# Diffusion step in fp32 on one core: the first layer's latent projection in two halves of the features, woven into the loading of the modulation blocks, and three unread products in place of nine

## The reference

```python
mod_s = jnp.split(modulation(c, w_mod[layer], b_mod[layer]), MOD_CHUNKS, -1)    # silu(c) @ w_mod + b_mod
hs = modulate(rms_norm(xs, g_norm1[layer]), mod_s[0], mod_s[1])                 # h * (1 + scale) + shift
proj = h @ w_in                                  # layer 0: 256 + 128 + 32 latent columns, then 2 x 512 of the conv branch
cq, ckv, k_rope, glu = proj[..., :256], proj[..., 256:384], proj[..., 384:416], proj[..., 416:]
```

## Time and profile before

| what | us |
|---|---|
| median of 3 runs | 1579.98 |
| lowest and highest run | 1578.2, 1583.39 |
| the profiled execution, its own time | 1586.21 |
| its span (the first to the last instruction) | 1584.0 |
| TensorE busy | 1442.6 (91%) |
| VectorE, ScalarE, GpSimd busy | 807.4, 474.6, 201.6 |
| mean granted clock of TensorE | 0.973 of full speed |
| DMA | 268.68 MB, mean 170 GB/s |

### The profile page before, as it was taken

How to read it: one execution, slowest core, us unless ns; L and a number is a source line. 1 busy time by engine, 2 the same in 40 slices (tenths; PEclk the granted TensorE clock), 3 DMA queues, 4 the chain that set the end, 5 groups by cost and what they waited for, 6 DMA issues and landing times.

```text
span 1584.0 us, 34040 instructions
## 1 busy us (share of the span) xinstructions
PE 1442.6 (91%) x14714; PEld 1016.4 (64%) x14714; DVE 807.4 (51%) x1586; ACT 474.6 (30%) x1066; POOL 201.6 (13%) x201
## 2 busy tenths in 40 slices
PE   3999989999999998778898999988989999999994
PEld 2555567745588886556676776766755444788883
DVE  1278678734443433535566665665644525343432
ACT  2201655512100000544554544554531202000000
POOL 2200020100312121131011010110100002112111
PEclk9999999999999999889998998999999999999998
DMA  9764573232899999522101201111012433999994
GB/s 344 263 224 134 171 244 123 79 120 102 294 344 345 338 342 352 160 72 56 45 22 46 64 22 46 45 42 59 6 57 74 156 106 142 318 341 344 338 291 112
DMA packets 165158, 268.68 MB, mean 170 GB/s; under 512 B 7697, under 2 KB 107289, under 8 KB 164337
## 3 DMA queue, kind: packets, MB, share of 16 engines
q1 hardware_dynamic: 149008, 206.29, 38.5%
q0 software_dynamic: 16000, 60.23, 13.0%
HBM read 237.45 MB, written 36.36 MB: 173 GB/s over the span
## 4 chain that ended last, share of the span: by engine, by line
PE 75%; DVE 9%; issue 5%; DMA 4%; ACT 3%; DVEq 1%; SPq 1%; POOL 0%; ACTq 0%; POOLq 0%
PE psum L1679 14%; PE psum L928 9%; PE psum L2125 8%; PE psum L1690 7%; PE psum L580 5%; PE psum L2187 4%; PE psum L2137 2%; PE psum L334 2%; PE psum L2684 2%; PE psum L1392 2%; PE psum L489 2%; PE psum L1671 2%; PE psum L944 2%; DMA arena<-in_w_mod 1%; PE psum L955 1%
## 5 line engine op out<-in xcount | busy, mean ns | idle before, releaser
L2125 PE MATMUL psum<-hT,ring 128*128 128x384 f32 (+1 forms) x736 | 241.9, 453 | 1.0 <-ACTq L213 0.7
L2125 PEld LDWEIGHTS psum<-hT,ring 128*128 128x128 f32 x736 | 128.3, 194 | 34.5 <-issue 2.1
L1679 PEld LDWEIGHTS psum<-arena,ring 128*128 128x128 f32 x1152 | 131.1, 192 | 12.4 <-issue 10.4
L1679 PE MATMUL psum<-arena,ring 128*128 128x128 f32 x1152 | 131.9, 275 | 4.8 <-DVE arena L1720 4.8
L1758 DVE TENSOR_TENSOR arena<-arena,psum 128x256 f32<-128x256 f32 x34 | 14.3, 421 | 211.7 <-PE psum L1679 211.7
L737 DVE SCALAR_TENSOR_TENSOR arena<-arena,params_sb 128x655 f32<-128x655 f32 x120 | 106.1, 906 | 5.6
L2187 PEld LDWEIGHTS psum<-arena 32*32 32x32 f32 x5120 | 55.7, 111 | 65.3 <-issue 37.6
L2187 PE MATMUL psum<-arena 32*32 32x32 f32 x5120 | 64.9, 200 | 29.6 <-issue 18.5
L1620 POOL DMA_INDIRECT ysum<-arena,small x34 | 53.9, 1587 | 285.5 <-DVE arena L1728 284.9
L1741 ACT ACTIVATE arena<-psum 128x256 f32<-128x256 f32 x34 | 13.1, 384 | 222.6 <-PE psum L1679 222.6
L928 PE MATMUL psum<-ring,arena 128*128 128x512 f32 x160 | 72.6, 608 | 1.0 <-ACTq L213 1.0
(11 more groups left out here) (476 smaller groups left out, 2626.8 us busy)
## 6 DMA issues: line engine op xcount, KB each, us to landing
arena<-in_w_mod SPq DMA_DIRECT2D x18, 1024.0 KB, 5.2
ring<-in_m_w_gate SPq DMA_DIRECT2D x18, 1024.0 KB, 11.2
ring<-in_m_w_up SPq DMA_DIRECT2D x18, 1024.0 KB, 16.8
ring<-in_m_w_down SPq DMA_DIRECT2D x18, 1024.0 KB, 15.1
ring<-in_w_mod SPq DMA_DIRECT2D x17, 1024.0 KB, 5.5
modN<-in_m_w_down SPq DMA_DIRECT2D x16, 1024.0 KB, 15.9
ring<-in_c_w_in SPq DMA_DIRECT2D x24, 512.0 KB, 6.7
arena<-in_m_w_gate SPq DMA_DIRECT2D x8, 1024.0 KB, 13.6
```

Source lines behind the costliest of these rows:

```text
L1679: m = pe.matmul(bank((2, 4)[half] + (1, 3)[half] * q, P, f * P), gu_slot[s][:, c0:c0 + P], xgT[:, q, k, :], start=(k == 0), stop=(k == KC ...
L2125: m = pe.matmul(bank(un % 2, w), ring[:, s, c0k:c0k + P], hT[:, k, o:o + w], start=(k == 0), stop=(k == KC - 1))
```

## The change

1. The order of the loads: blocks 0 and 2 of the modulation weights (shift and scale of the features 0 to 511), then the latent weights of those features (0.85 MB), then blocks 1 and 3, then the other half of the latent weights. The latent weights have a slot of their own, so they no longer wait for a product.
2. TensorE multiplies blocks 0 and 2 and turns them into columns, then transposes tiles and multiplies the first four feature chunks of each tile (`latent_half(pe, t, 0)`). The products of blocks 1 and 3 and the columns from them are put in between. The other four chunks follow for all five tiles at the end. Each tile accumulates in a bank of its own, 0 to 4.
3. The first half of a tile is modulated out of PSUM by ScalarE (even tiles) or VectorE (odd tiles); the other engine copies the second half into `hT` as it is. When the second half of `mcol` is there, VectorE modulates it in place, chunk by chunk over all 640 rows: 8 instructions, with one count of `mod_k` for each chunk.
4. All five `latent_copy` stand behind the barrier `norm0a`, which TensorE now reports to in the midst of its products.
5. `unread_products` in the combination: 3 in place of 9.

Semaphore totals and reused semaphores are adapted. Nothing else of the 1584 us is touched.

```diff
@@ mod_sp
-            for b in range(NCB):
-                sp.dma_start(first_slot[b].rearrange("p (k n) -> p k n", k=KC), w[:, :, b * 512:(b + 1) * 512]).then_inc(S(f"mod_w{b}"), 16)
+            for half, sem in enumerate(("in0_w_lat", "in0_w_u")):
+                for b in (half, 2 + half):
+                    sp.dma_start(first_slot[b].rearrange("p (k n) -> p k n", k=KC), w[:, :, b * 512:(b + 1) * 512]).then_inc(S(f"mod_w{b}"), 16)
+                sp.dma_start(ring[:, 0, 4 * half * LAT:4 * (half + 1) * LAT].rearrange("p (k n) -> p k n", k=4),
+                             w_in[:, 4 * half:4 * half + 4, 0:LAT]).then_inc(S(sem), 16)
@@ mod_pe
-            for b in range(NCB):
-                if b == NCB - 2:
-                    norm_tile_pe(pe, 0, 0)
-                    norm_tile_pe(pe, 0, 1)
-                pe.wait_ge(S(f"mod_w{b}"), 16)
-                block_rows(pe, first_slot[b], bank(6, P, b * P), 0, KC).then_inc(S("mod_col_mm"), 1)
-            rows_to_columns(pe, 0)
-            arrive(pe, "pe")
+            first_rows(pe, 0)
+            first_rows(pe, 2)
+            rows_to_columns(pe, 0, (0, 2), 2)
@@ norm0_act
-            act.wait_ge(S("mod_col_mm"), NCB)
-            act.copy(col_rows[0], bank(6)).then_inc(S("mod_vec_ev"), 1)
+            act.wait_ge(S("mod_col_mm"), 2)
+            act.copy(halves(col_rows[0])[:, :, 0, :], halves(bank(6))[:, :, 0, :]).then_inc(S("mod_vec_ev"), 1)
...
+            for t in range(NT):
+                act.wait_ge(S("norm_tr"), 2 * t + 1 + t % 2)
+                if t % 2:
+                    m = act.copy(hT_half(t, 1), bank(late_bank(t)).rearrange("p (a b) -> p a b", a=4))
+                else:
...
+            act.wait_ge(S("mod_col_mm"), 4)
+            act.copy(halves(col_rows[0])[:, :, 1, :], halves(bank(6))[:, :, 1, :]).then_inc(S("mod_vec_ev"), 1)
@@ norm0_dve
+            mod_columns(dve, 0, (1,), 3)
+            dve.wait_ge(S("in_hT_act"), NT)
+            dve.drain()
+            for k in range(4, KC):
+                for c, part in ((0, slice(0, P)), (1, slice(P, T))):
+                    m = dve.tensor_scalar(hT[:, k, part], hT[:, k, part], mcol[:, 0, 1, k, c:c + 1], mcol[:, 0, 0, k, c:c + 1], ALU.mult, ALU.add)
+                m.then_inc(S("mod_k"), 1)
@@ norm_pe
+            first_tile_pe(pe, 0)
+            first_tile_pe(pe, 1)
             pe.wait_ge(S("in0_w_lat"), 16)
-            for t in range(NT):
-                latent_product(pe, t)
-                if t + 2 < NT:
-                    norm_tile_pe(pe, 0, t + 2)
+            latent_half(pe, 0, 0)
+            first_tile_pe(pe, 2)
+            latent_half(pe, 1, 0)
+            first_tile_pe(pe, 3)
+            first_rows(pe, 1)
+            latent_half(pe, 2, 0)
+            first_tile_pe(pe, 4)
+            first_rows(pe, 3)
+            latent_half(pe, 3, 0)
+            rows_to_columns(pe, 0, (1, 3), 3)
+            arrive(pe, "pe")
+            latent_half(pe, 4, 0)
+            pe.wait_ge(S("in0_w_u"), 16)
+            for t in range(NT):
+                latent_half(pe, t, 1)
@@ in0_sp
-            sp.wait_ge(S("mod_col_mm"), 1)
-            sp.dma_start(slot(0, KC, LAT), w_in[:, :, 0:LAT]).then_inc(S("in0_w_lat"), 16)
@@ in0_act
-            for t in range(NT - 2, NT):
+            for t in range(NT):
                 latent_copy(act, t)
@@ gates_pe
-            unread_products(pe, 9)
+            unread_products(pe, 3)
```

More of the change, by code:

```diff
@@ L335, in block_rows, with rows_to_columns, first_rows @@
             return m
-        def rows_to_columns(pe, l):
-            pe.wait_ge(S("mod_vec_ev"), 2 + l)
-            for b in range(NCB):
+        def rows_to_columns(pe, l, blocks, evicted):
+            pe.wait_ge(S("mod_vec_ev"), evicted)
+            for b in blocks:
                 m = pe.transpose(bank(7, P, b * P), col_rows[l][:, b * P:(b + 1) * P], ident)
             m.then_inc(S("mod_vecT"), 1)
+        def first_rows(pe, b):
+            pe.wait_ge(S(f"mod_w{b}"), 16)
+            block_rows(pe, first_slot[b], bank(6, P, b * P), 0, KC).then_inc(S("mod_col_mm"), 1)
         def mod_pe(pe):
@@ L442, in latent_copy @@
             act.wait_ge(S("in0_lat_mm"), t + 1)
-            act.copy(proj[:, t, :], bank(t % 2, LAT)).then_inc(S("in0_lat_ev"), 1)
+            act.copy(proj[:, t, :], bank(t, LAT)).then_inc(S("in0_lat_ev"), 1)
         def scale_rows(dve, o, t):
@@ L456, in norm0_dve @@
             dve.drain()
-            for t in range(4):
-                scale_rows(dve, 0, t)
-            mod_columns(dve, 0)
+            scale_rows(dve, 0, 0)
+            scale_rows(dve, 0, 1)
+            mod_columns(dve, 0, (0,), 2)
             dve.drain()
             for t in range(NT):
[L462 to L466, removed]
-                m.then_inc(S("in_hT_dve"), 1)
-                if t == 2:
-                    scale_rows(dve, 0, 4)
+                dve.wait_ge(S("norm_tr"), 2 * t + 2 - t % 2)
+                if t % 2:
+                    c = cond_of(t)
+                    for k in range(4):
+                        m = dve.tensor_scalar(hT[:, k, tok(t)], bank(t, P, k * P), mcol[:, 0, 1, k, c:c + 1], mcol[:, 0, 0, k, c:c + 1],
+                                              ALU.mult, ALU.add)
+                else:
+                    m = dve.tensor_copy(hT_half(t, 1), bank(late_bank(t)).rearrange("p (a b) -> p a b", a=4))
+                m.then_inc(S("in_hT_dve"), 1)
+                if t + 2 < NT:
+                    scale_rows(dve, 0, t + 2)
+            mod_columns(dve, 0, (1,), 3)
[5 more added lines that the diff above has]
+                m.then_inc(S("mod_k"), 1)
             barrier(dve, "dve", "norm0a")
@@ L481, in norm_tile_pe, with first_tile_pe @@
                 m.then_inc(S("norm_tr"), 1)
-        def latent_product(pe, t):
-            pe.wait_ge(S("in_hT_act"), t + 1)
-            pe.wait_ge(S("in_hT_dve"), t + 1)
-            if t >= 2:
-                pe.wait_ge(S("in0_lat_ev"), t - 1)
-            for k in range(KC):
-                m = pe.matmul(bank(t % 2, LAT), hT[:, k, tok(t)], ring[:, 0, k * LAT:(k + 1) * LAT],
+        def first_tile_pe(pe, t):
+            pe.wait_ge(S("norm_h"), t + 1)
+            if t == NT - 1:
+                pe.wait_ge(S("in_hT_act"), NT - 1)
+            for k in range(4):
+                m = pe.transpose(bank(t, P, k * P), hbuf[:, t % 2, k * P:(k + 1) * P], ident)
+            m.then_inc(S("norm_tr"), 1)
+            if t >= 2:
+                pe.wait_ge(S("in_hT_act" if t % 2 else "in_hT_dve"), t - 1)
+            for j in range(4):
+                k = 4 + j
+                m = pe.transpose(bank(late_bank(t), P, j * P), hbuf[:, t % 2, k * P:(k + 1) * P], ident)
+            m.then_inc(S("norm_tr"), 1)
@@ L490, in latent_product, with latent_half @@
+        def latent_half(pe, t, half):
+            if half == 0:
+                pe.wait_ge(S("in_hT_dve" if t % 2 else "in_hT_act"), t + 1)
+            for k in range(4 * half, 4 * half + 4):
+                if half and t == 0:
+                    pe.wait_ge(S("mod_k"), k - 3)
+                m = pe.matmul(bank(t, LAT), hT[:, k, tok(t)], ring[:, 0, k * LAT:(k + 1) * LAT],
                               start=(k == 0), stop=(k == KC - 1))
-            m.then_inc(S("in0_lat_mm"), 1)
+            if half:
+                m.then_inc(S("in0_lat_mm"), 1)
@@ L989, in attn0_pe @@
                 if u == 16:
-                    rows_to_columns(pe, 1)
+                    rows_to_columns(pe, 1, range(NCB), 4)
                 if u == 18:
-                    pe.wait_ge(S("mod_col"), 2)
+                    pe.wait_ge(S("mod_col"), 3)
                 if u == 33:
```

48 lines of the change are left out of this document (27 added, 21 removed).

## The result

| | before | with the change |
|---|---|---|
| median of 8 runs, us | 1580.53 | 1569.61 |
| lowest and highest run | 1578.15, 1589.43 | 1561.69, 1575.45 |
| ratio, 95% interval | | 0.9923 (0.9905 to 0.9942) |
| the profiled execution, its own time | 1586.21 | 1568.32 |
| its span | 1584.0 | 1566.2 |

The change takes 0.77% off, 12.2 us by the ratio, 10.9 by the medians. The forecast was 1568.6, 11.4 us less than 1579.98; the range 1564.5 to 1576.0.

A forecast was written before the change was run, and what follows sets the result against it. TensorE was taken to have little to do until 39.95 us, waiting on the fourth modulation block, and too much after. Start 7.9 plus combination 3.5 gave 11.4 off 1579.98: 1568.6 us, range 1564.5 to 1576.0.

The forecast's parts named there:

- The start: Kernel start to end of latent products: first latent product near 29.4 us, end at 64.4 against 72.36, 7.9 us gained.
- the five tiles: Latent products of five tiles on TensorE at full clock: 5 x 5.60 = 28.0 us.
- the drain: TensorE's drain of its report to the barrier amid the latent products: 0 to 0.3 us, taken as 0.2.
- the second block's products: TensorE's products of the second modulation block, at the start: 3.60 us from 22.40, ending at 26.00 as before.
- The clock at the first half tile: First latent half tile at the low clock level would cost 1.8 us more; taken as 0, 1.8 kept for the range.
- The combination: Six of nine unread products dropped; VectorE modulates tile 0 at 648.61 against 652.14: 3.5 us, bounds -1.7 and 6.2.
- the fall of the earlier trace: TensorE's clock fall in the combination, 9 us or more after the unread products end, assumed to move along with them.
- B: Rival: the clock falls earlier, over the key projections, taking back the unread products' gain; gain 7.9, 1572.1 us; chance 0.18.
- C: Rival: loads do not land in turn, second block whole 6.6 us later; gain 4.8, 1575.2 us; chance 0.07.
- D: Rival: the start's gain is lost in the expert stage if transfers set its end; 3.5 left, 1576.5 us; chance 0.09.
- E: Rival: slower, TensorE's clock low in the woven latent stretch; half of 35 us low loses 17.5, 1586 us; chance 0.04.
- The estimate of 0.45 a chunk: VectorE's in-place modulation by the skill's formula: about 0.45 us a chunk; bounds 1.15 and half of that.

The follow-up runs named there:

- the other profile of the old start: Kernel before with three unread products in the combination in place of nine, the start unchanged: 1577.29 us, ratio 0.9982; GLU products at 74.8 us.
- The kernels with the early root: The change with ScalarE's square-root table loaded early and the root first for two tiles (ratio 0.9931); two more also start TensorE earlier (0.9898, 0.994).
- the last experiment: The change with early root, TensorE at work earlier and two unread products ahead of block 2: 1569.64 us against 1580.49, ratio 0.994.
- the order of loads: The change with modulation blocks 0, 1, 2 loaded ahead of the first latent weights, then block 3: 1577.36 us, ratio 0.9968.
- The twenty: The change with each chunk's in-place modulation in five instructions of 128 columns, 20 in place of 8: a single run, 1569.13 us, no ratio.

## Why the prediction was right

**The start, 7.9 forecast, 7.4 measured.** The first latent product was put at 29.4 and stood at 29.39; the end of the run of TensorE was put at 64.4 and stood at 64.89. The term that was too small is the five tiles. By the chain, latent work came to 28.85, not 28.0: half of 5.60 is 2.80, and the first half tile took 3.03, the one behind the transposes of tile 2 took 2.80, the two behind a block 2.99 each, and the last six halves 17.04, or 2.84 each. Blocks 1 and 3 took 1.86 each, not 1.97, the drain 0.1, not 0.2. Transfers, ScalarE and VectorE were covered as said: no wait for them between 29.39 and 64.89. That 7.9 came so near to 7.4 is in part luck: against the other profile of the old start, in which the fourth block was slow as well, the gain is 9.2.

**One step was right for another reason.** I had the second block's products end at 26.0, at 3.60; here they took 1.93 and ended at 24.4. It made no difference, because ScalarE's root and VectorE's two row scalings end at 27.3 either way. I had named VectorE as the later one, but not that the squares and the table load behind X had become the chain. The kernels with the early root show that this chain is the longer one by 0.3 us with the block's products at 3.59 and by 1.9 at 1.93.

**The clock at the first half tile.** Taken as 0 of 0 to 1.8, and 0 it was, in every profile of the new start.

**The combination, 3.5 forecast.** VectorE's wait of 3.5 is gone, as said. By the pair nine and three with the same start it is 3.7 to the key projections; by the first modulation, 3.1, since the late products took 0.47 longer in this profile. That the number of products does not set the clock on the key projections held too: with the new start, nine, six, three and none all have 5.24 and 3.50 there. The slow 5.18 came with nine in the kernel before and with three in the last experiment (661.13 to 666.31), and not elsewhere. But I let the fall of the earlier trace rows move along with the products, and with the change it did not come: the granted clock reads 1.00 from 637 us to the end of the key projections. The 1.7 us on the second of them are thus no part of the 3.5; they are in one profile of the kernel before and not in the other kernel with its start.

**The rivals.** B: with three products nothing was taken back. With none the clock did fall earlier, as B has it, but beside VectorE's work, and the stage has the same 25.7 us. C: wrong, by the order of loads; the 6.6 us of its working was the right size (6.5), and what a late block costs is 5.9. The Trainium skill ("DMA: Bandwidth & Descriptors", the section on queues, rings and completion order), which was cited for it, allows both; the landings here are in turn, at 22.5, 29.0 and 37.0 by the waits of TensorE in three kernels. D: wrong, 7.4 us at the GLU products and 8.0 at the end of the experts, although the DMA share there is 1.06, as in the earlier trace rows. E: no low stretch between 29.39 and 64.89.

The Trainium skill ("VectorE: DVE Perf Modes", the section on the TRN2 errata) has a fixed cost for each instruction with an SBUF source. The twenty and the eight agree with that: 2.28 us for twelve more instructions over the same columns, 0.19 each. The estimate of 0.45 a chunk by its formula was low; 2.94 / 4 = 0.74 was measured, within my bounds of 0.58 and 1.15. It cost nothing, since it lay beside latent products.

## What to carry to other kernels

Where a chain begins with a transfer, ask which part of it the first useful product needs, load the parts in that order, and put the work that they allow between the later parts: without the order 5.9 of the 7.4 us were lost, without the work in between 3.3 (the two overlap and do not add up). Work that keeps an engine warm is free only up to the moment when its next operand is there; read that moment from the trace (the scaled rows at 646.57) and count products up to it. A profile shows the clock of one execution: the second block's products cost 3.60 in the profile that was read and 1.93 in most others. When a difference of a few us is in question, compare stages that the edit does touch; stages that it does not touch scatter by as much.

## What the runs showed of the hardware

The heads stage, with the same code in every kernel, took 533.4 to 540.2 us in fourteen profiles. Its time at the low level, an estimate from the granted clock of 5 us stretches, is 51, 51 and 48 us in the three profiles with the longest stage and 38 in the shortest, but 51 also in one of 536.7. That the clock makes the scatter is thus likely in part, and not shown. The median of one kernel, the change, was 1569.61 on one occasion and 1573.52 on another, with 1580.53 and 1584.19 for the kernel before beside it; only the ratios (0.9923, 0.9928) agree. The record of the granted clock reads 1.00 from the start of the span, while a block's products take 3.59 there and 1.93 later: before its first recorded fall it does not tell the level, and durations have to. With the kernel before, the products of the same block took 1.97 in one profile and, behind a shorter wait, 3.44 in another.
